# Normalising attention probabilities in place on VectorE and turning them by transposes, in a two-layer hybrid decoder step

## What is computed

```
# 8 query heads, 2 key/value heads, head size 64; at most 128 keys per query are kept
score = where(key position <= query position, sum_h wi[h] * relu(qi[h] . ki) * IDX_SCALE, NEG_BIG)
top_val, top_idx = top_k(score, 128)
logits = einsum('bqngd,bqknd->bqngk', q, k[top_idx]) * ATTN_SCALE
logits = where(valid, logits, NEG_BIG)
p = softmax(logits, axis=-1)
o = einsum('bqngk,bqknd->bqngd', p, v[top_idx])
```

## Time and profile before

| | us |
|---|---|
| median of 3 runs | 2732.87 |
| lowest and highest | 2732.65 and 2733.94 |
| the profiled execution, its own time | 2733.12 |
| span of the profiled execution | 2731.0 |
| TensorE busy (matmul) | 2668.8 |
| VectorE busy | 922.7 |
| ScalarE busy | 824.3 |
| GpSimd busy | 1102.7 |

### The profile page before, as it was taken

The page is one execution under the profiler, slowest core; times in us unless marked ns, Lnnn a source line. Parts: engine busy times, 40 slices in busy tenths (PEclk is TensorE's granted clock), DMA queues, the critical chain, the costliest instruction groups (busy, mean ns, idle before and its releaser), DMA issues. The chain is left out here.

```text
span 2731.0 us, 54017 instructions
## 1 busy us (share of the span) xinstructions
PE 2668.8 (98%) x22428; PEld 2535.7 (93%) x22428; DVE 922.7 (34%) x2323; ACT 824.3 (30%) x1313; POOL 1102.7 (40%) x886
## 2 busy tenths in 40 slices
PE   6999999999999999999999999999999999999998
PEld 4999998999888989999989999989998889899998
DVE  4111113266784441111131111134677824311111
ACT  2321222222454233212233212232234532332221
POOL 4434345233323364344453444542333224544443
PEclk9999999999999999999999999999999999999999
DMA  6334345212223344332533332641122125122222
GB/s 245 138 124 147 139 165 179 104 48 84 77 68 94 109 142 139 124 112 90 185 137 139 120 97 92 200 153 63 63 88 70 55 93 184 66 93 92 93 89 81
DMA packets 107056, 312.90 MB, mean 115 GB/s; under 512 B 18476, under 2 KB 45130, under 8 KB 89434
## 3 DMA queue, kind: packets, MB, share of 16 engines
q1 hardware_dynamic: 97952, 290.60, 31.5%
q10 hardware_dynamic: 8906, 19.44, 2.0%
HBM read 299.56 MB, written 10.66 MB: 114 GB/s over the span
## 5 line engine op out<-in xcount | busy, mean ns | idle before, releaser
L949 POOL TENSOR_TENSOR w_lo<-raw,w_hi 128x512 fp32r<-128x512 f32 (+1 forms) x800 | 1010.5, 1293 | 1594.2 <-ACT w_hi L1023 1546.6
L2162 PE MATMUL bank<-h_hi,w_hi 128*128 128x260 f32 x3744 | 1067.5, 285 | 2.8 <-ACT silu_g L1070 2.4
L2163 PE MATMUL bank<-h_hi,w_lo 128*128 128x260 f32 x3744 | 1053.7, 281 | 0.0
L2164 PE MATMUL bank<-h_lo,w_hi 128*128 128x260 f32 x3744 | 1053.5, 281 | 0.0
L2162 PEld LDWEIGHTS bank<-h_hi,w_hi 128*128 128x128 f32 x3744 | 703.2, 188 | 37.6 <-issue 35.6
L2163 PEld LDWEIGHTS bank<-h_hi,w_lo 128*128 128x128 f32 x3744 | 703.6, 188 | 0.0
L2164 PEld LDWEIGHTS bank<-h_lo,w_hi 128*128 128x128 f32 x3744 | 703.3, 188 | 0.0
L1023 ACT CAST w_hi<-raw 128x2048 fp32r<-128x2048 f32 (+3 forms) x219 | 376.5, 1719 | 481.8 <-PE bank L2164 377.5
L2162 PE MATMUL bank<-mid_hi,w_hi 128*128 128x260 f32 x1232 | 351.2, 285 | 0.0
L2164 PE MATMUL bank<-mid_lo,w_hi 128*128 128x260 f32 x1232 | 348.5, 283 | 0.0
L2163 PE MATMUL bank<-mid_hi,w_lo 128*128 128x260 f32 x1232 | 348.4, 283 | 0.0
(11 more groups left out here) (334 smaller groups left out, 3342.4 us busy)
## 6 DMA issues: line engine op xcount, KB each, us to landing
raw<-in_w SPq DMA_DIRECT2D x120, 1024.0 KB, 4.9
raw<-in_w SPq DMA_DIRECT2D x64, 512.0 KB, 4.3
raw<-in_w SPq DMA_DIRECT2D x32, 768.0 KB, 4.3
ada_ring<-in_ada SPq DMA_DIRECT2D x82, 256.0 KB, 5.2
raw<-in_w SPq DMA_DIRECT2D x32, 640.0 KB, 4.0
ada_ring<-in_ada SPq DMA_DIRECT2D x57, 320.0 KB, 5.3
ada_ring<-in_ada SPq DMA_DIRECT2D x57, 192.0 KB, 5.3
ada_low<-in_ada SPq DMA_DIRECT2D x20, 256.0 KB, 4.8
```

Source lines behind the costliest of these rows:

```text
L949: last = pool.tensor_tensor(w_lo[j][:, cols], raw[j][:, cols], w_hi[j][:, cols].bitcast(F32), ALU.subtract)
L2162: mm(out, wh(wb), xh(xb), start=(n == 0), stop=False)
L2163: mm(out, wl(wb), xh(xb), start=False, stop=False)
L2164: last = mm(out, wh(wb), xl(xb), start=False, stop=(n == len(blocks) - 1))
```

## The change

`diagonals` and its four tiles are gone from ScalarE. VectorE gets a new function, `normalise`, that runs right after the reciprocal of each step: it waits for its own reciprocal and multiplies the two `probs` tiles of the step (128 x nk each) in place by the row's reciprocal. TensorE's turn waits for these two instructions rather than for the diagonals, and each block is now a transpose with the identity as the moving operand. The semaphore `diag_ready` becomes `scaled_probs`; `own_diag_ready` is only renamed.

```diff
-        diag = [area(f"diag{j}", [P, P], 80096 + 512 * j) for j in range(4)]
...
-            def diagonals(l, step):
-
-                p = step % 4
-                act.wait_ge(inv_ready, STEPS * l + step + 1)
-                for i in range(2):
-                    h = p + 4 * i
-                    s.activation(diag[2 * (step % 2) + i][:], ident[:], ACT.Copy, scale=row_inv[:, h:h + 1])\
-                     .then_inc(diag_ready, 1)
-
...
-                    if step < STEPS:
-                        diagonals(l, step)
...
+            def normalise(l, step):
+
+                t, p = divmod(step, 4)
+                nk = (t + 1) * P
+                for i in range(2):
+                    h = p + 4 * i
+                    tile = probs[2 * (step % 2) + i]
+                    v.tensor_scalar(tile[:, 0:nk], tile[:, 0:nk], row_inv[:, h:h + 1], None, ALU.mult)\
+                     .then_inc(scaled_probs, 1)
+
...
                         v.reciprocal(row_inv[:, p:NH:4], row_sum[:, p:NH:4]).then_inc(inv_ready, 1)
+                        dve.wait_ge(inv_ready, STEPS * l + step + 1)
+                        normalise(l, step)
...
-                pe.wait_ge(diag_ready, 2 * (STEPS * l + step + 1))
+                pe.wait_ge(scaled_probs, 2 * (STEPS * l + step + 1))
...
-                        last = mm(out[:, ks], probs[2 * (step % 2) + i][:, ks], diag[2 * (step % 2) + i][:],
-                                  start=True, stop=True)
+                        last = nc.tensor.transpose(out[:, ks], probs[2 * (step % 2) + i][:, ks], ident[:])
```

More of the change, by code:

```diff
@@ L625, in build @@
         inv_ready = sem("inv_ready")
-        diag_ready = sem("diag_ready")
+        scaled_probs = sem("scaled_probs")
         turn_full = sem("turn_full")
@@ L639, in build @@
         s_probs_ready = sem("s_probs_ready")
-        own_diag_ready = sem("own_diag_ready")
+        own_scaled_probs = sem("own_scaled_probs")
         blk_ready = sem("blk_ready")
@@ L2057, in sample_attention @@
                 v.tensor_scalar(own_diag[:], ident[0:NB * NH, 0:NB * NH], prob_s[:, PAST:LVIS], None, ALU.mult)\
-                 .then_inc(own_diag_ready, 1)
+                 .then_inc(own_scaled_probs, 1)
                 src, done = wait_side(dve, l, "s_probT")
@@ L2726, in sample_attention @@
                                         ident[0:NB * NH, 0:NB * NH])
-                pe.wait_ge(own_diag_ready, l + 1)
+                pe.wait_ge(own_scaled_probs, l + 1)
                 mm(out[0:NB, 2 * NB * NH:3 * NB * NH], gather_heads[:], own_diag[:], start=True, stop=True)\
```

## The result

| | before | after |
|---|---|---|
| median of 18 runs each, us | 2733.78 | 2737.94 |
| lowest and highest | 2731.65 and 2735.24 | 2736.63 and 2740.69 |
| the profiled execution, its own time | 2733.12 | 2737.93 |
| span of the profiled execution | 2731.0 | 2735.8 |

The ratio after/before is 1.0017, 95% interval 1.001 to 1.0024. The changed kernel is slower by some 4 us where 3 us less were forecast.

The account below looks back on a forecast made before the run. TensorE bounds nearly everywhere, VectorE in steps 0 to 11 of the prompt attention. TensorE's 9.7 us a layer shrank to 3.9 behind VectorE, to 1.5 with the port: 2733.1 - 3.0 = 2730.1, forecast 2730 us, 8-in-10 range 2719 to 2740.

Parts of the forecast that it names:

- TensorE's gain: Prompt attention's turns: a transpose replaces two passes, 0.121 us a block, 9.7 us a layer, 19.4 in the program.
- The rival of a transpose that isn't pipelined: At the turns, each transpose costs its 272 ns record against 224 for two passes: 2746 us; transposes not cheaper, chance 0.04.
- The price of the scalings: VectorE's new scalings: 0.29, 0.35, 0.42 and 0.49 us for the four widths, 8.0 us in steps 0 to 11.
- The shared port: VectorE's scalings wait for GpSimd's pieces near steps 0, 3, 5 and 8: 2.4 of 3.8 us a layer taken.
- The rival with the port at its full price at four steps: Both scalings wait a whole piece in steps 0, 3, 5, 8: +5.1 us a layer, 2743; within the slower case, 0.14.
- VectorE as the bound of steps 0 to 11: VectorE's 67.65 us of work plus 8.0 fills the stretch; TensorE waits at turns 1, 3, 11 and step 4's index products.
- my pass with the port: Starts of the prompt attention carried forward step by step: -3.9 us a layer without port holds, -1.5 with those taken.
- What holds the turn of step 11: Step 11's scaled probabilities, ready at 825.05 us at the earliest, hold TensorE's turn: 1.4 us sooner instead of 5.1, before port.
- After step 11 VectorE has slack, and 4.6 us come through, less about 0.5: Later prompt attention: the other 38 blocks' gain of 4.6 us shows, less 0.5 for step 12's late maxima.
- VectorE's chain takes back more than TensorE gains: Rival, steps 0 to 11: port holds make the kernel slower once VectorE carries 3.9 us more; 2735 to 2743, chance 0.14.

Follow-up runs that it names:

- e1: The changed kernel without the two VectorE scalings of each step, prompt probabilities left unnormalised; 2720.06 us, ratio 0.9945 to the kernel before.
- e2: The changed kernel with ScalarE, not VectorE, scaling the two probability tiles in place; 2717.05 us, ratio 0.9943 to the kernel before.
- e4: The changed kernel with `yc_lo` of values unit 4 moved from step 12 to after the third search round of step 11; 2732.57 us, ratio 1.0001 to before.
- the best version: The changed kernel with ScalarE scaling, `yc_lo` moved ahead and GpSimd pieces of 256 columns instead of 512; 2710.23 us, ratio 0.9912 to the kernel before.

## Why the prediction was wrong, step by step

**TensorE's gain: right.** Line 2640 has one record a block, 160 in all. Eight transposes and the logits behind them start 1.02 us apart, where 16 passes and the logits behind them took 2.00 before (weight loads, kernel before and then after):

```profile
842.41 1.88 PEld L2640 LDWEIGHTS bank<-diag,probs 128*128 128x128 f32 x16
844.41 0.30 PEld L2628 LDWEIGHTS bank<-rotT 64*128 64x128 f32 x4
```
```profile
837.26 0.86 PEld L2640 LDWEIGHTS bank<-ident,probs 128*128 128x128 f32 x8 [0.17 <-issue]
838.28 0.30 PEld L2628 LDWEIGHTS bank<-rotT 64*128 64x128 f32 x4 [0.17 <-issue]
```

That is the 0.97 us for 8 blocks of the sum, within 0.01. The rival of a transpose that isn't pipelined is refuted. The Trainium skill ("TensorE: Matmul & The Clock Gate", "PE-mode transpose") gives about 275 ns, measured in one kernel, for a 128x128 transpose of bf16. The records of the 32-bit ones here last as long, 273 ns at the median, but their starts lie 0.10 to 0.13 us apart, and that is what they cost.

**The price of the scalings: right**, 0.28 us at the least for 128 columns, 0.35 and 0.42 for 256 and 384, and 0.48 for 512, half of an undisturbed pair with its overlap.

**The shared port: right in size.** The pairs of steps 0 and 3 took 1.69 and 1.57 us, where 0.48 is their plain time: 1.21 and 1.09 more, 2.3 together, against the 2.4 that I took. The rival with the port at its full price at four steps did not happen. By the Trainium skill ("SBUF — State Buffer", "Who interferes with whom") the engine that loses the shared pair of ports waits for the winner's whole instruction. The fall of step 15's pair from 2.95 to 1.45 us as GpSimd's pieces were halved agrees; step 0's, 1.69 to 1.54, does not show it.

**VectorE as the bound of steps 0 to 11: right.** The waits at the turns of steps 1 and 3 and at the index product of step 4 are there (1.33, 1.16 and 0.38 us of idle time of its matmuls), and the one at step 6 grew by 0.51, 3.4 in all. That last one is 1.22 us in e1 and e2 too, so it belongs to the faster turn and not to VectorE. By the logits of step 12 TensorE was 0.87 us ahead of before; the rest of the gain of 5.1 had gone, most of it into these waits, as the prediction said. Step 11's scalings ended at 827.03, 79.51 us from the first logits, where the turn had started at 78.11. That is 1.4 us late; my pass with the port implied 2.6.

**What holds the turn of step 11: wrong.** This is the step that failed. The prediction let TensorE arrive at that turn when step 11's probabilities are scaled, 2.6 us later than before with the port. I followed only the semaphores that the diff touches, reciprocal and scalings, and let TensorE walk freely up to the turn. It can't: a product of the filling ahead of the turn needs a bank that VectorE frees by `yc_lo`, and `yc_lo` stands behind the scalings and the maxima of step 12. It ended at 828.59, 81.07 us from the first logits, 1.56 later than the scalings. The remaining products, at half the clock, took the turn to 82.59. So the turn came 4.48 us later than before: 1.4 of them for the scalings, as foreseen in kind, and 3.1 for `yc_lo` and what followed it.

**"After step 11 VectorE has slack, and 4.6 us come through, less about 0.5": near.** From the start of that turn to the end it took 35.31 us before and 31.74 after, a gain of 3.57 and not 4.1; some 0.6 of it went into the low clock in the turn itself. Predicted: 2.6 - 4.1 = -1.5 a layer. Measured: 4.48 - 3.57 = +0.91.

The rival "VectorE's chain takes back more than TensorE gains" named the right engine and the right sign, with a threshold of 3.9 us more than the 8.0 in steps 0 to 11. The mechanism was another: not more work on VectorE, but a release queued behind it.

**The clock: missing.** The prediction has no term for it. Of the 4.48 us at the turn 0.64 are the stretch at 1.2 GHz behind the gap, and at least 0.61 more lie behind the turn's start. e4 shows what this term is worth: with `yc_lo` out of the way the attention is 113.00 us, only 0.42 under before and not 1.5, and its window loses 1.7 us to the low clock. By these numbers, as an estimate, the release cost 1.3 us a layer and the clock up to 1.7; without both the layer would be some 2.1 us shorter than before, as forecast in sign.

**The rest of the program: missing.** It was taken as unchanged and cost 2 to 3 us, about as much as its stretches at 1.2 GHz add. By sums: 1.9 us in the two attentions and 2.9 outside make the 4.8 between the spans. What stays open is why the kernel before meets fewer of these stretches. That the gaps at 905 us are the same is shown; what else decides was not found, and no run here isolates it.

## What to carry to other kernels

Before pricing a shift, list every semaphore that the bound engine waits for in the stretch, the releases of its banks too, with the time between the release and the instruction that needs it: a release with 0.05 us of slack shows as no wait at all. New work on an engine is worth what it delays behind it in the queue, not its own duration; the dearer instruction on the engine with room was the cheap one (564 ns on ScalarE, 0.3 us a layer in the end; 351 to 418 ns on VectorE, 9 us a layer). And a stall of the bound engine costs more than its length if its clock falls after it.

## What the runs showed of the hardware

- Transposes of 32-bit 128x128 blocks start 0.10 to 0.13 us apart at granted clock 1.00; the product with a diagonal takes 0.224 us for the same block (16 passes in 1.79 us).
- Behind an idle time of 4.57 us TensorE's granted clock was 0.50 for some 3 us in both layers, in the second from 0.6 us after the restart on. A shorter pair of gaps (1.05 and 0.68 us) near 905 us was followed by a fall in both traces of the kernel after and in neither of the kernel before. A gap of 2.45 us near 1000 us was followed by one in the trace of the kernel before and by none in that of the kernel after.
- A scaling with one per-row operand takes 278 ns for 128 columns and 351 for 256, where one with constants took 294 for 256.
- The length of GpSimd's instructions sets how long VectorE's products in the recurrence are held at the most (1584 ns with pieces of 512 columns, 854 with 256). Of the three lengths tried the middle one was best: pieces of 256 columns beat 512 by 6 us in the kernel before, and 128 lose 5 us to 256 in the best version, GpSimd's busy time rising from 1103 to 1227 and 1478 us.
